# Expert matmuls in 64-token halves with 32-token strips behind them, and the down projection loaded in 16 KB rows

## The reference, cut to what matters

```
def swiglu(h, w_gate, w_up, w_down):
    return (jax.nn.silu(h @ w_gate) * (h @ w_up)) @ w_down

def moe_swiglu(h, router_w, w_gate, w_up, w_down):
    logits = (xf @ router_w).astype(jnp.float32)
    top_logits, top_idx = lax.top_k(logits, TOP_K)
    gates = jax.nn.softmax(top_logits, axis=-1)
    ...
    ys = lax.map(expert_block, (xs, blk_e)).reshape(P, D) * slot_gate[:, None]
    return jnp.zeros((N, D), h.dtype).at[slot_tok].add(ys).reshape(B, S, D)
```

## Time and profile before

| what | value |
|---|---|
| median of 3 runs | 1378.35 us |
| the profiled execution | 1377.18 us |
| its span, first to last instruction | 1375.3 us |
| granted TensorE clock, mean over the span | 0.988 of 2.4 GHz |
| TensorE matmul records | 18,759 |
| DMA packets, and what they moved | 127,063; 418.88 MB |
| first matmul of the expert stage | 483.5 us |

### The profile page before, as it was taken

The page is one execution under the profiler, slowest core; times in us unless marked ns, Lnnn a source line. Parts: engine busy times, 40 slices in busy tenths (PEclk is TensorE's granted clock), DMA queues, the critical chain, the costliest instruction groups (busy, mean ns, idle before and its releaser), DMA issues.

```text
span 1375.3 us, 39781 instructions
## 1 busy us (share of the span) xinstructions
PE 1303.9 (95%) x18759; PEld 927.0 (67%) x18759; DVE 342.7 (25%) x664; ACT 326.9 (24%) x699; POOL 0.2 (0%) x4
## 2 busy tenths in 40 slices
PE   6999999999999899999999999899989989999997
PEld 6786999997877656665666665565666565566565
DVE  5666555555585500010010000010001001001000
ACT  5665544444576300010000010010000001000000
POOL 0000000000000000000000000000000000000000
PEclk9999999999999999999999999999999999999999
DMA  9903454463511469999999999999999999999991
GB/s 363 390 24 123 157 190 143 141 239 130 184 62 61 185 258 373 373 341 399 403 408 408 401 408 407 395 408 409 378 409 407 386 405 387 407 402 408 408 365 41
DMA packets 127063, 418.88 MB, mean 305 GB/s; under 512 B 3376, under 2 KB 8112, under 8 KB 126768
## 3 DMA queue, kind: packets, MB, share of 16 engines
q1 hardware_dynamic: 126896, 416.29, 78.6%
HBM read 415.23 MB, written 1.05 MB: 303 GB/s over the span
## 4 chain that ended last, share of the span: by engine, by line
PE 87%; DVE 3%; ACT 3%; issue 3%; DMA 2%; SPq 1%; DVEq 0%; ACTq 0%
PE ps L816 37%; PE ps L803 18%; PE ps L502 7%; PE ps L504 7%; PE ps L503 7%; DMA ring<-moe_g 2%; PE ps L892 2%; PE ps L835 1%; PE ps L484 1%; SPq L461 1%; DVE scratch L1359 1%; PE ps L630 1%; ACT scratch L1012 1%; PE ps L635 1%; PE ps L638 1%
## 5 line engine op out<-in xcount | busy, mean ns | idle before, releaser
L816 PE MATMUL ps<-ring,xgT 128*32 128x256 f32 (+1 forms) x8096 | 404.0, 358 | 18.0 <-issue 17.6
L816 PEld LDWEIGHTS ps<-ring,xgT 128*32 128x32 f32 x8096 | 256.0, 111 | 158.3 <-issue 27.3
L803 PE MATMUL ps<-ring,hidT 128*32 128x256 f32 x3840 | 221.4, 382 | 11.3 <-issue 10.2
L803 PEld LDWEIGHTS ps<-ring,hidT 128*32 128x32 f32 x3840 | 126.1, 110 | 94.5 <-issue 21.5
L1634 DVE TENSOR_TENSOR hT<-ps,hT 128x768 f32<-128x768 f32 (+3 forms) x32 | 24.7, 771 | 634.5 <-PE ps L816 634.5
L816 PE MATMUL ps<-more_ring,xgT 128*32 128x256 f32 (+1 forms) x2656 | 124.8, 344 | 6.5 <-issue 3.2
L1467 DVE TENSOR_TENSOR d_lo<-ring,d_hi 128x1024 fp32r<-128x1024 f32 x82 | 100.3, 1225 | 95.0 <-ACT d_hi L1120 94.7
L1161 ACT ACTIVATE hidT<-ps 128x768 f32<-128x768 f32 (+3 forms) x32 | 21.2, 662 | 432.2 <-PE ps L835 432.2
L1120 ACT ACTIVATE d_hi<-ring 128x1024 fp32r<-128x1024 f32 x82 | 87.3, 1064 | 111.9 <-PE ps L504 111.9
L816 PEld LDWEIGHTS ps<-more_ring,xgT 128*32 128x32 f32 x2656 | 81.0, 110 | 46.7 <-issue 9.8
L502 PE MATMUL ps<-hT_hi,d_hi 128*128 128x256 f32 x352 | 99.7, 283 | 1.0 <-DVE hT_lo L1247 1.0
(11 more groups left out here) (243 smaller groups left out, 1204.3 us busy)
## 6 DMA issues: line engine op xcount, KB each, us to landing
ring<-moe_d SPq DMA_DIRECT2D x46, 2048.0 KB, 21.1
ring<-moe_u SPq DMA_DIRECT2D x45, 2048.0 KB, 24.2
ring<-moe_g SPq DMA_DIRECT2D x41, 2048.0 KB, 23.1
more_ring<-moe_g SPq DMA_DIRECT2D x15, 2048.0 KB, 24.1
more_ring<-moe_u SPq DMA_DIRECT2D x11, 2048.0 KB, 24.2
more_ring<-moe_d SPq DMA_DIRECT2D x10, 2048.0 KB, 19.5
ring<-w_in SPq DMA_DIRECT2D x6, 2048.0 KB, 10.9
ring<-dense_g SPq DMA_DIRECT2D x5, 2048.0 KB, 7.8
```

Of the source, the lines that this page charges most:

```text
L803: ins = pe.matmul(ps[q * STRIP:(q + 1) * STRIP, 4 + t // 2, t % 2 * T:(t % 2 + 1) * T], hidT[:, c // 2 % 2, x0:x0 + STRIP], w[:, j * D + q ...
L816: ins = pe.matmul(ps[q * STRIP:(q + 1) * STRIP, b0 + b, c0:c0 + wide], xgT[:, k, t * STRIP:(t + 1) * STRIP], w[:, i * cols + q * wide:i * ...
```

## The change

- The first 64 tokens are one "half" each way: two column tiles of 64, each with all 64 tokens and half of the columns (512 of a 1024-column block in g and u units, 512 of the 1024 outputs in d units). Tokens 64 to 95, in big experts only, stay in four column tiles of 32. Within a unit all k blocks of the halves come first and then all of the strips.
- Down-projection units are loaded so that partition p holds rows 4p to 4p + 3 of the 512, which are 16 KB in one piece. For this the hidden columns have to arrive on partitions in the same order: the transposes in `hidden_T` take every fourth (or second) column of `hid`, and where the columns of a chunk of 512 are spread over two or four column tiles, the weights are read in steps: pairs of elements out of every four for the halves of the last chunk and for the strips of the others, one element out of every four for the strips of the last chunk.
- `pick_g` holds the gates twice for the halves and four times for the strips (128 + 128 columns for 3 x 128), so `gates_T` has four transposes in place of six in a big expert and two in place of four in a small one. `scatter` uses row tiles of 64 for the halves and of 32 for the strips.

The diff, with the buffers' and the helper's lines in it:

```diff
...
+HALF, HALVES = 64, 2
 STRIP, STRIPS = 32, 4
...
 SMALL_AT = (1, 3, 6)
...
             pick = sb_stage("pick", [P, TT, GROUP], F32R)
-            pick_g = sb_stage("pick_g", [P, TT, BIG, STRIPS, STRIP])
-            pick_gT = sb_stage("pick_gT", [P, BIG * TT * P])
+            pick_g = sb_stage("pick_g", [P, TT, 2 * P])
+            pick_gT = sb_stage("pick_gT", [P, 2 * TT * P])
             xn_hi = sb_stage("xn_hi", [P, TT, D], F32R)
...
             more_ring = sb_stage("more_ring", [P, MORE_SLOTS, UNIT])
...
             return LITTLE if g == 0 and s in SMALL_AT else BIG
+        def groups(g, s):
+            return strips(g, s) - 1 if g or s < NE - 1 else 2
...
             return strips(g, s - 1 if g == 0 else s)
...
                         src = (moe_g if kind == "g" else moe_u)[0, e, h * rows:(h + 1) * rows, cols]
-                    sp.dma_start(moe_slot(g, s, m).rearrange("p (k n) -> p k n", n=src.shape[-1]),
-                                 src.rearrange("o (k p) n -> p (o k) n", p=P)).then_inc(
+                    src = (src.rearrange("o (p k) n -> p (o k) n", p=P) if kind == "d"
+                           else src.rearrange("o (k p) n -> p (o k) n", p=P))
+                    sp.dma_start(moe_slot(g, s, m).rearrange("p (k n) -> p k n", n=src.shape[-1]), src).then_inc(
                                      slot_loaded[moe_slot_no(g, s, m)], 16)
...
             expert_units(0)
...
                         for j in range(CH // P):
                             if c < NCH - 1:
-                                quarter, part, parts = c % 2 * 2 + j // 2, j % 2, 2
+                                x0 = j * P + c % 2 * HALF
                             else:
-                                quarter, part, parts = j, 0, 1
-                            for t in range(nt):
-                                x0 = (t * parts + part) * P + quarter * STRIP
-                                for q in range(STRIPS):
-                                    ins = pe.matmul(ps[q * STRIP:(q + 1) * STRIP, 4 + t // 2, t % 2 * T:(t % 2 + 1) * T],
-                                                    hidT[:, c // 2 % 2, x0:x0 + STRIP],
-                                                    w[:, j * D + q * T:j * D + (q + 1) * T],
-                                                    start=c == 0 and j == 0 and t % 2 == 0,
-                                                    stop=c == NCH - 1 and j == CH // P - 1, skip_group_check=True)
+                                x0 = j % 2 * P + j // 2 * HALF
+                            for q in range(HALVES):
+                                ins = pe.matmul(ps[q * HALF:(q + 1) * HALF, 4, :], hidT[:, c // 2 % 2, x0:x0 + HALF],
+                                                w[:, j * D + q * CH:j * D + (q + 1) * CH], start=c == 0 and j == 0,
+                                                stop=c == NCH - 1 and j == CH // P - 1, skip_group_check=True)
+                        for j in range(CH // P if nt == BIG else 0):
+                            if c < NCH - 1:
+                                x0 = (4 + j % 2) * P + (c % 2 * 2 + j // 2) * STRIP
+                            else:
+                                x0 = 2 * P + j * STRIP
+                            for q in range(STRIPS):
+                                ins = pe.matmul(ps[q * STRIP:(q + 1) * STRIP, 5, 0:T], hidT[:, c // 2 % 2, x0:x0 + STRIP],
+                                                w[:, j * D + q * T:j * D + (q + 1) * T], start=c == 0 and j == 0,
+                                                stop=c == NCH - 1 and j == CH // P - 1, skip_group_check=True)
                     else:
-                        cols = GU_COLS[c]
-                        wide, b0 = cols // STRIPS, 0 if kind == "g" else 2
-                        for i in range(UNIT // cols):
-                            k = h * (UNIT // cols) + i
-                            for t in range(nt):
-                                b, c0 = divmod(t * wide, CH)
-                                for q in range(STRIPS):
-                                    ins = pe.matmul(ps[q * STRIP:(q + 1) * STRIP, b0 + b, c0:c0 + wide],
-                                                    xgT[:, k, t * STRIP:(t + 1) * STRIP],
-                                                    w[:, i * cols + q * wide:i * cols + (q + 1) * wide],
-                                                    start=k == 0 and c0 == 0, stop=k == KD - 1, skip_group_check=True)
+                        cols, ks = GU_COLS[c], UNIT // GU_COLS[c]
+                        wide, b0 = cols // HALVES, 0 if kind == "g" else 2
+                        for i in range(ks):
+                            k = h * ks + i
+                            for q in range(HALVES):
+                                ins = pe.matmul(ps[q * HALF:(q + 1) * HALF, b0, 0:wide], xgT[:, k, 0:HALF],
+                                                w[:, i * cols + q * wide:i * cols + (q + 1) * wide] if cols > CH else
+                                                w[:, i * cols:(i + 1) * cols].rearrange("p (n v e) -> p v n e", v=2, e=2)[:, q],
+                                                start=k == 0, stop=k == KD - 1, skip_group_check=True)
+                        b, c0 = divmod(wide, CH)
+                        for i in range(ks if nt == BIG else 0):
+                            k = h * ks + i
+                            for q in range(STRIPS):
+                                ins = pe.matmul(ps[q * STRIP:(q + 1) * STRIP, b0 + b, c0:c0 + wide // 2],
+                                                xgT[:, k, HALF:HALF + STRIP],
+                                                w[:, i * cols:(i + 1) * cols].rearrange("p (u n v e) -> p u v n e", u=cols // CH, v=2, e=2)[
+                                                    :, q // 2, q % 2] if cols > CH else
+                                                w[:, i * cols:(i + 1) * cols].rearrange("p (n v) -> p v n", v=STRIPS)[:, q],
+                                                start=k == 0 and c0 == 0, stop=k == KD - 1, skip_group_check=True)
                     ins.then_inc(pe_done, pe_p.step((g, s, "unit", n)))
...
                 def hidden_T(s, it, c):
...
                         b = j // 4 + (6 if c < NGU - 1 else 0)
-                        ins = pe.transpose(ps[:, b, j % 4 * P:(j % 4 + 1) * P], hid[:, j * P:(j + 1) * P], ident)
+                        if c == NGU - 1:
+                            part = (hid[:, 0:2 * P].rearrange("p (n e) -> p e n", e=2)[:, j] if j < 2
+                                    else hid[:, 2 * P:3 * P])
+                        elif j < 4:
+                            part = hid[:, 0:4 * P].rearrange("p (n e) -> p e n", e=4)[:, j]
+                        else:
+                            part = hid[:, 4 * P:6 * P].rearrange("p (n e) -> p e n", e=2)[:, j - 4]
+                        ins = pe.transpose(ps[:, b, j % 4 * P:(j % 4 + 1) * P], part, ident)
                     ins.then_inc(pe_done, pe_p.step((g, s, "hid_T", c)))
...
                     pe.wait_ge(act_done, at((g, s, "hidT", 1), it))
-                    for t in range(strips(g, s)):
+                    for t in range(groups(g, s)):
                         for a in range(TT):
                             j = t * TT + a
-                            ins = pe.transpose(ps[:, 6 + j // 4, j % 4 * P:(j % 4 + 1) * P],
-                                               pick_g[:, a, t, :, :].rearrange("p q i -> p (q i)"), ident)
+                            ins = pe.transpose(ps[:, 6, j * P:(j + 1) * P], pick_g[:, a, t * P:(t + 1) * P], ident)
                     ins.then_inc(pe_done, pe_p.step((g, s, "pick_g_T")))
...
                 def expert(s, it=None):
...
-                for t in range(nt):
-                    for a in range(TT):
-                        for q, bank in enumerate(SCATTER_BANKS):
-                            rows_q = slice(q * STRIP, (q + 1) * STRIP)
-                            ins = pe.matmul(ps[:, bank, a * T:(a + 1) * T],
-                                            pick_gT[rows_q, (t * TT + a) * P:(t * TT + a + 1) * P],
-                                            y[rows_q, t * T:(t + 1) * T], start=t == 0 and a == 0, stop=t == nt - 1,
-                                            skip_group_check=True)
+                for a in range(TT):
+                    for n in range(2):
+                        for q in range(HALVES):
+                            rows_q = slice(q * HALF, (q + 1) * HALF)
+                            ins = pe.matmul(ps[:, SCATTER_BANKS[q * 2 + n], a * T:(a + 1) * T],
+                                            pick_gT[rows_q, a * P:(a + 1) * P], y[rows_q, n * T:(n + 1) * T],
+                                            start=a == 0, stop=nt == LITTLE, skip_group_check=True)
+                for a in range(TT if nt == BIG else 0):
+                    for q, bank in enumerate(SCATTER_BANKS):
```

(18 more changed lines are left out.)

## The result

The change made the kernel slower by 0.6%: 1387.41 us (median of 8 runs) against 1377.68 for the kernel before in the same rounds, ratio 1.0063 with a 95% interval of 1.0050 to 1.0077. The forecast was 1366.5. The profiled run took 1387.72 us, span 1385.8.

The account below looks back on a forecast made before the run. Transfers and TensorE were taken as bounds within 6 us of each other; after gains and costs expert 7 starts at 1232.1, its transfer deciding by a hair, and takes 119.8: -11.5 us, 1366.5 predicted, range 1351 to 1388.

Parts of the forecast that it names:

- Strided reads: Half of the reads and some transposes' weight loads read in steps: taken as free, bounds 0 and double.
- Single-word strips: Last chunk's 32-wide strips reading 4 bytes of 16: taken as free; at double, 2 x 1.7 us per big expert.
- Pairs in wide units: Third strip in 12 wide units of a big expert, reading 8 bytes of every 16: taken as free.
- Strided weight loads of the transposes: Four of six transposes' weight loads read in steps: taken as free; at double, 12 x 0.11 us per big expert.
- Rival 3: Reads of one word in 16 bytes take double, TensorE decides before expert 7: +2.9 us, about 1381; chance 0.17.
- Rival 4: Strided reads cost more, pairs pay a quarter too: about 1410 us, deciding from 3.7 us per big expert; chance 0.10.
- Fewer instructions: TensorE's waits for instructions in last-chunk units after 906 us: all 22.1 us go, bounds 11 and 22.1.
- Streaming: Columns times passes unchanged; two 64-wide tiles run side by side like four of 32; 0.2 us less per expert from transposes.
- Change of tile width: TensorE going between 64-wide and 32-wide tiles: 36 x 0.13 = 4.7 us per big expert, bounds 0 and 9.4.
- Rows of 16 KB: Third-matrix transfers take 4.98 us a unit for 5.14, 0.16 less, between bounds of 4.81 and 5.19.
- rival 1: Long rows bring nothing, third-matrix units stay at 5.14 us and transfers decide: -5.4 us, about 1373; chance 0.13.

Follow-up runs that it names:

- e6_no_single_reads: Changed kernel with only the last chunk's gate and up strips reading their 128 columns contiguously instead of one word in four; 1368.63 us, ratio 0.9938 to the kernel before.
- e4_hybrid: Kernel before with two 64-wide halves only in the last chunk's gate and up units, all reads contiguous, 4 KB rows; 1363.57 us, ratio 0.9897.
- e3_before_rows16: Kernel before with one line changed: third-matrix units loaded in 16 KB rows, strips kept, no strided read; 1372.8 us, ratio 0.9964.
- e5_serpentine: e1_last_plain with the order of halves and strips turned in every other unit of a big expert, so width stays over the boundary; 1360.4 us, ratio 0.9873.
- e1_last_plain: Changed kernel with no strided read in the last chunk, its third-matrix unit in 4 KB rows; 1368.81 us, ratio 0.9937 to the kernel before.

## Why the prediction was wrong

**The step that failed** is "Strided reads": "I take it as free, the bounds are 0 and double". It was the forecast's only cost with no near row, and the end that I took was the wrong one. Term by term, for a big expert:

- Single-word strips: bound 2 x 1.7 = 3.4, taken as 0; measured 2 x 1.9 = 3.8 (e6_no_single_reads). With the last chunk's pairs a unit is 7.55 for a forecast 5.44: 4.2 for two.
- Pairs in wide units: taken as 0; measured 12 x 0.09 = 1.1. These two (4.2 and 1.1) make up the 5.3 us by which expert 4 missed; experts 5 and 7 missed by 5.7 and 5.9.
- Strided weight loads of the transposes: bound 1.3, measured 0.11 for six, some 0.4.

What then followed from that step: TensorE, not the transfer, sets expert 7's start, by the 5.9 us between the data's landing at 1240.4 and 1246.3. The landing itself was forecast for 1232.1. It came 8.3 us later, and later than in the kernel before (1238.4 in the trace; the forecast's 1239.2 went by the median time of an issue), although each transfer of the third matrix was faster: its slots came free later. The forecast had the two resources side by side, each with its own sum, and left out that a slower TensorE also holds the transfers back. Experts 4 to 7 need 465.8 us for the 449.3 of the forecast. 16.5 of the 22 us between the forecast's 1365.7 for a profiled run and 1387.7 lie here; the start of expert 4 holds 3.6 more and the tail 1.8.

**Rival 3 was the right mechanism**; the Trainium skill's rule in "SBUF — State Buffer", Door 1, that a 16-byte line needs two hits for full bandwidth, agrees in whom it charges (3.74 against 1.89) and nearly in whom it spares: pairs at 1.95 for 1.86 pay a twentieth, though by the rule they pay nothing. The page states no size for the loss; the double was the rival's. That the 16-byte line is the reason is argued, since no run tells it from four tiles reading the same 16 bytes. The rival's time, 1380.1 for a profiled run (1381 against the median), was 7.6 short of 1387.7. It took the transfer to decide expert 4's start at 902.6. The transfer did land at 903.1, but experts 0 and 2 pay the same 5 us each, the stage began 3.1 late, and TensorE came at 906.2; the pairs and the tail of the kernel carried the rest. I gave it 0.17, though no row spoke against it and a rule spoke for it. Rival 4's condition (over 3.7 us in each big expert) was met, but mainly by single words, not by pairs; its quarter was a twentieth.

**What held.** *Fewer instructions*: no "issue" wait is left in the last chunks, and e4_hybrid shows that those waits were worth having out. Expert 6, which has no third strip, fell from 87.8 to 82.3, forecast 81.7; 1.7 of the 5.9 us that the forecast put down to instructions there was the clock of 0.68 shown under e3_before_rows16, so that this number held partly by luck. *Streaming*: two 64-wide tiles run side by side as four 32-wide do; 5.44 for a unit is 5.18 plus the two changes of width. *Change of tile width*: 0.13 forecast, 0.12 to 0.15 measured in e5_serpentine; the Trainium skill's sentence in "TensorEngine Tiling (Array Packing)", Key Properties, that a change of mode drains the engine, agrees with a price for 64 to 32 as well, though a drain as such is seen in no trace. *Rows of 16 KB*: 4.98 forecast, 4.9 measured, between the bounds of 4.81 and 5.19; rival 1's premise falls. The windows of the earlier trace rows answer with fewer records and no wait, as forecast:

```profile
1031.20:1120.80 89.60, 89.60 (x776) 34.20 (x772) 6.26 (x11) 5.46 (x7) 0.00 (x0) 1.00 1.00 392
...
600.00:625.00 25.00, 25.00 (x184) 10.66 (x184) 3.61 (x8) 3.58 (x8) 0.00 (x0) 1.00 0.90 345
```

TensorE is at 89.6 of 89.6 in both kernels; only the expert's length tells that the same busy time now does less. The DMA share of the second window is 0.90 as before: the forecast took 1 us off for fewer instruction blocks and less idle DMA in experts 0 and 1, and the blocks are fewer, but the idle share is as it was.

## What to carry to other kernels

A layout that is better for the transfer is paid by the engine that reads it: before rows are made longer, write down the stride in which every matmul will read its moving operand, and price one word in 16 bytes as double and two as a twentieth more, as they cost here. Where two resources are within 1% of each other, put each remedy only where its own resource decides: fewer and wider matmuls in the chunk that runs out of instructions, long rows in the experts that wait for data. And when a step has no near row and its two ends decide the sign, the forecast should be its dear end or should be said to be a coin.

## What the runs showed of the hardware that I had not expected

Pairs of words at 8 bytes of every 16 aren't free: 1.95 against 1.86 in strips of 32, 3.77 against 3.58 to 3.60 in halves of 64, the same 5%. Loading weights with a stride costs little: 0.92 for 0.81 us in six transposes, four of which read every fourth word and two every second.

The granted clock can drop round the two microseconds for which TensorE waits for the copy of the last result. The windows of the last scatter, in the kernel after, in e4_hybrid and in e1_last_plain, are

```profile
1373.00:1381.00 8.00, 5.65 (x32) 3.56 (x32) 0.44 (x1) 0.00 (x0) 0.00 (x0) 0.62 0.01 2
```

```profile
1354.60:1357.60 3.00, 2.87 (x48) 2.36 (x48) 0.04 (x1) 0.00 (x0) 0.00 (x0) 1.00 0.03 5
```

```profile
1356.40:1361.70 5.30, 3.55 (x32) 2.46 (x32) 0.00 (x0) 0.00 (x0) 0.00 (x0) 1.00 0.01 3
```

The clock is only part of it. In e4_hybrid the scatter takes 2.9 us at a clock of 1.00; in e1_last_plain it takes 5.3 at 1.00, of which TensorE is busy for 3.55 and waits 1.71 in one piece for instructions; in after it takes 6.6 at 0.62 with 0.9 of such waits; before it took 4.65 at 0.64. From the last unit to the end that is 10.3 us in e4_hybrid, 12.5 in e1_last_plain and 13.8 in after. After the same wait of some 2 us the clock fell in after and not in the other two, and no experiment tried what decides that. It is a large part of what single profiles of these kernels differ by, which is why the verdicts above rest on medians and on the durations of single units.
